# Seven-product pairs for the third block's queries, keys and values

## What is computed

```python
proj = rms_norm(x, pre_norm_w) @ w_in          # 2048 -> sb_q, sb_k, sb_v, sb_gate (1024 each),
                                               #         c_q 512, c_kv 256, k_rope 64, mla_gate 1024
o_a = stick_breaking_attention(sb_q, sb_k, sb_v)              # 8 heads of 128
o_b = chunk_causal_softmax_attention(q_mla, k_mla, v_mla)     # from c_q and c_kv, 8 heads of 192
y = concat(o_a * silu(sb_gate), o_b * silu(mla_gate)) @ w_out
return x + rms_norm(y, post_norm_w)
```

## Time and profile before

| | before |
|---|---|
| median of three runs | 1258.91 us (1258.35 to 1259.91) |
| the profiled execution, its own time | 1258.95 us |
| its span, first to last instruction | 1256.9 us |
| PE busy, matmuls | 1248.4 us (99%), 5918 |
| DVE busy | 833.9 us (66%) |
| ACT busy | 782.2 us (62%) |
| POOL busy | 205.0 us (16%) |
| mean granted clock of TensorE | 1.000 |

### The profile page before, as it was taken

One profiled execution on the slowest core, in us unless ns is written; L12 is line 12 of the kernel. 1 busy time (PEld: TensorE's weight loads), 2 busy tenths in 40 slices (PEclk: granted clock), 3 DMA queues, 4 the chain that ended last, 5 costly groups with the idle time before them and its releaser, 6 DMA issues.

```text
span 1256.9 us, 16105 instructions
## 1 busy us (share of the span) xinstructions
PE 1248.4 (99%) x5918; PEld 1040.5 (83%) x5918; DVE 833.9 (66%) x1341; ACT 782.2 (62%) x1230; POOL 205.0 (16%) x149
## 2 busy tenths in 40 slices
PE   9999999999999999999999999999999999999998
PEld 8888888888888888888888888889988888888886
DVE  5497898476657667898787765656544445576545
ACT  5798798765547556655657774456644454666543
POOL 1499999900000000000000010000000000000000
PEclk9999999999999999999999999999999999999999
DMA  9899999944566656667555545567655556655563
GB/s 348 271 256 251 271 252 247 268 159 142 184 191 184 193 184 184 201 190 213 162 157 158 155 156 199 183 181 184 178 165 164 157 161 184 195 162 161 182 194 133
DMA packets 133564, 243.85 MB, mean 194 GB/s; under 512 B 12144, under 2 KB 22512, under 8 KB 133360
## 3 DMA queue, kind: packets, MB, share of 16 engines
q1 hardware_dynamic: 129600, 229.40, 58.9%
q0 software_dynamic: 3600, 13.11, 5.3%
q10 hardware_dynamic: 288, 0.32, 0.1%
HBM read 227.60 MB, written 2.10 MB: 183 GB/s over the span
## 4 chain that ended last, share of the span: by engine, by line
PE 94%; POOL 2%; DVE 1%; ACT 1%; DMA 1%; issue 0%; DVEq 0%; ACTq 0%
PE PS L1768 28%; PE PS L1770 28%; PE PS L1769 27%; PE PS L1687 2%; PE PS L1706 2%; PE PS L1800 1%; POOL w_more L581 1%; PE PS L1802 1%; PE PS L1801 1%; PE PS L1955 1%; DMA tap_products<-tap_products 1%; POOL w_lo L581 1%; PE PS L1851 0%; PE PS L1890 0%; PE PS L1853 0%; PE PS L1852 0%
## 5 line engine op out<-in xcount | busy, mean ns | idle before, releaser
L1133 DVE TENSOR_TENSOR w_lo<-w_raw,w_hi 128x1024 fp32r<-128x1024 f32 (+2 forms) x339 | 407.9, 1205 | 300.7 <-ACT w_hi L637 299.9
L637 ACT ACTIVATE w_hi<-w_raw 128x1024 fp32r<-128x1024 f32 (+2 forms) x383 | 399.0, 1044 | 332.0 <-PE PS L1770 302.2
L1768 PE MATMUL PS<-w_hi,actB_hi 128*128 128x512 f32 (+1 forms) x736 | 292.4, 397 | 0.0
L1770 PE MATMUL PS<-w_hi,actB_lo 128*128 128x512 f32 (+1 forms) x736 | 284.8, 387 | 0.0
L1769 PE MATMUL PS<-w_lo,actB_hi 128*128 128x512 f32 (+1 forms) x736 | 284.1, 386 | 0.0
L1768 PE MATMUL PS<-w_hi,actA_hi 128*128 128x512 f32 x724 | 283.7, 392 | 0.0
L1770 PE MATMUL PS<-w_hi,actA_lo 128*128 128x512 f32 x724 | 282.1, 390 | 0.0
L1769 PE MATMUL PS<-w_lo,actA_hi 128*128 128x512 f32 x724 | 281.8, 389 | 0.0
L1770 PEld LDWEIGHTS PS<-w_hi,actB_lo 128*128 128x128 f32 x736 | 138.1, 188 | 28.8
L1770 PEld LDWEIGHTS PS<-w_hi,actA_lo 128*128 128x128 f32 x724 | 135.9, 188 | 28.8
L1769 PEld LDWEIGHTS PS<-w_lo,actB_hi 128*128 128x128 f32 x736 | 138.4, 188 | 25.6
(11 more groups left out here) (336 smaller groups left out, 1258.2 us busy)
## 6 DMA issues: line engine op xcount, KB each, us to landing
w_raw<-in_a_w_in SPq DMA_DIRECT2D x95, 512.0 KB, 5.8
w_raw<-in_w_in SPq DMA_DIRECT2D x88, 512.0 KB, 3.7
w_raw<-in_w_kv SPq DMA_DIRECT2D x64, 512.0 KB, 3.8
w_raw<-in_b_w_in SPq DMA_DIRECT2D x64, 512.0 KB, 3.8
w_raw<-in_a_w_out SPq DMA_DIRECT2D x32, 512.0 KB, 3.7
w_raw<-in_b_w_out SPq DMA_DIRECT2D x32, 512.0 KB, 3.7
w_raw<-in_w_out SPq DMA_DIRECT2D x32, 512.0 KB, 4.2
tap_products<-tap_products POOLq DMA_DIRECT2D x25, 512.0 KB, 8.3
```

Of the source, the lines that this page charges most:

```text
L637: nc.scalar.activation(split_slot(u)[0][:, f:2 * w], w_raw[:, RAW_SLOT[u], f:2 * w], ACT.Copy)\
L1133: V.tensor_tensor(wl, w_raw[:, RAW_SLOT[u], f:2 * w], wh.bitcast(F32), ALU.subtract)\
L1768: T.matmul(bank, ah, wh[:, kk, :], start=(first or opens_last and tok == 1) and kk == 0, stop=False)
L1770: ins = T.matmul(bank, al, wh[:, kk, :], start=False, stop=last and kk == 1)
```

## The change

It adds a second table, `LATE`: seven more pairs by seven products, three in sb_q (units 318, 322, 326), two in sb_k (336, 340), two in sb_v (352, 356), each with its partner unit behind it. These groups use seven PSUM banks, other ones for each group: `col1` for the first chunk, `col2` for the second, `more` for three products by themselves. The softmax heads keep to bank 6 (transposes too). For this:

- `late_acts` (DVE, steps 291 to 295, ACT in step 294): whole activations and their four sums of six K tiles, operations of 1536 or 384 elements, in parts.
- `late_differences` (DVE, steps 297 to 301, ACT in step 300, ahead of the hi parts of c_q): the difference of the two tiles of positions for the other 12 K tiles, 1536 elements each. The plain units of the second chunk of each group use it for `tok` 0 (`late_diff`), since one product of each pair is summed into the bank of `tok` 1 and is added to both.
- ACT reads one bank after a group's last pair, DVE joins (`join_late`) and scales and adds at the end (`finish_late`), in place of ACT's evacuations. For sb_v both halves are finished in step 362.
- The transposes of sb_q stand at steps 332 and 333, those of sb_k at 348 and 349, through the group's `col2`.
- The row maxima and exponentials of a softmax head stand behind the joins and the split of their step; on DVE `differences` come behind them.

The number of loads and their bytes stay. The core of the diff (the sums use `differences`, `differences_lo` and `seven_products` as they are, with other rooms; left out are the rooms, the semaphores' names and ACT's removed evacuations):

```diff
+LATE = [dict(c=C_SBQ, which="B", quads=(2, 4, 6), col1=(2, 3), col2=(0, 1), more=(4, 5, 7), turned="qu1"),
+        dict(c=C_SBK, which="B", quads=(3, 5), col1=(4, 5), col2=(2, 3), more=(7, 0, 1), turned="sq1"),
+        dict(c=C_SBV, which="B", quads=(3, 5), col1=(0, 1), col2=(4, 5), more=(7, 2, 3), turned="sk1")]
+LATE_BANKS = {}
+for g in LATE:
+    LATE_BANKS[g["c"]], LATE_BANKS[g["c"] + 1] = g["col1"], g["col2"]
+LATE_SUMS = max(len(g["quads"]) for g in LATE)
+LATE_PLAIN = 2 * min(len(g["quads"]) for g in LATE)
...
 KEEP_AT = [FIRST[C_V + 2] - 8, FIRST[C_Q] - 1]
+LATE_ACTS_AT, LATE_DIFF_AT = DONE[C_CQ - 1] + 3, DONE[C_CQ - 1] + 9
...
-BY_DVE = set(range(C_OUT, C_V)) | set(range(C_Q, C_ZB)) | set(range(C_OUTB, C_CQ)) | set(range(C_OUT2, NCH))
+BY_DVE = set(range(C_SBQ, C_MG)) | set(range(C_OUT, C_V)) | set(range(C_Q, C_ZB)) | set(range(C_OUTB, C_CQ)) | set(range(C_OUT2, NCH))
...
-            return PS[:, 2 * (c % 2) + tok, 0:(w or CHUNKS[c][2])]
+            bank = LATE_BANKS[c][tok] if c in LATE_BANKS else 2 * (c % 2) + tok
...
                         act.wait_ge(S["m_pt"], h + 1)
-                        nc.scalar.activation(probs_t[:, :], PS[:, 7, 0:384], ACT.Copy)\
+                        nc.scalar.activation(probs_t[:, :], PS[:, 6, 0:384], ACT.Copy)\
...
+                for n, g in enumerate(LATE):
+                    if u == g["units"][-1] + 2:
+                        act.wait_ge(S["units_done"], u)
+                        if n < 2:
+                            transposed(act, "sq1" if n else "ckv")
+                        for tok in range(TT):
+                            ins = nc.scalar.activation(late_join(g, 0, tok), PS[:, g["more"][0], :], ACT.Copy,
+                                                       scale=r_x2[:, tok:tok + 1])
+                        ins.then_inc(S["late_first"], 1)
...
+                h, b = divmod(u - MLA_FROM, MLA_STEP)
+                if 0 <= h < HEADS and b == 0:
+                    act.wait_ge(S["m_negmax"], h + 1)
+                    for tok, (f, e) in enumerate(((0, 128), (128, 384))):
+                        ins = nc.scalar.activation(work[:, h % 2, f:e], PS[:, 6, f:e], ACT.Exp,
+                                                   bias=neg_max[:, tok:tok + 1],
+                                                   accum_out=sums[:, tok:tok + 1])
+                    ins.then_inc(S["m_exp"], 1)
+                if u == LATE_ACTS_AT + 3:
+                    act.wait_ge(S["late_acts"], 1)
+                    chunk_done(act, C_CQ - 1)
+                    nc.scalar.activation(flat_a(hi)[:, 4 * NC:4 * NC + 512 * LATE_SUMS],
+                                         aux[:, 5 * H8:5 * H8 + 512 * LATE_SUMS], ACT.Copy)\
+                        .then_inc(S["late_acts_hi"], 1)
+                if u == LATE_DIFF_AT + 3:
+                    act.wait_ge(S["late_diff"], 1)
+                    at = 0
+                    for part in late_diffs(0):
+                        n = part.shape[-1]
+                        ins = nc.scalar.activation(part, aux[:, 4 * H8 + at:4 * H8 + at + n], ACT.Copy)
+                        at += n
+                    ins.then_inc(S["late_diff_hi"], 1)
+                for i, (m, dst, scale) in enumerate((("sq", sq_t, float(DH ** -0.5)), ("sk", sk_t, 1.0))):
+                    for j in range(2):
+                        if u == FIRST[LATE[i + 1]["c"]] + 2 + j:
+                            copy_pairs(f"{m}{j}", lambda b: dst[:, 4 * j + 2 * b:4 * j + 2 * b + 2, :], scale,
+                                       LATE[i]["col2"])
...
+            def late_acts(step):
+                n = 128 * LATE_SUMS
+                a = aux[:, 4 * H8:4 * H8 + 4 * n].rearrange("p (k t n) -> p k t n", t=TT, n=P)
+                a11, a12, a21, a22 = a[:, 0::2, 0, :], a[:, 1::2, 0, :], a[:, 0::2, 1, :], a[:, 1::2, 1, :]
+                sums_of = aux[:, 5 * H8:5 * H8 + 4 * n]
+                s1, s2, s3, s4 = (sums_of[:, i * n:(i + 1) * n].rearrange("p (q n) -> p q n", n=P) for i in range(4))
+                if step == 0:
+                    dve.wait_ge(S["lo_ready"], LO_NO["v3"] + 1)
+                    dve.wait_ge(S["on_ready"], HEADS)
+                    link(V.tensor_tensor(aux[:, 4 * H8:4 * H8 + 4 * n].rearrange("p (k s) -> p k s", s=SEQ),
+                                         hi["B"][:, 0:2 * LATE_SUMS, :].bitcast(F32),
+                                         lo["B"][:, 0:2 * LATE_SUMS, :].bitcast(F32), ALU.add))
+                if step == 1:
+                    link(V.tensor_tensor(s1, a21, a22, ALU.add))
+                    V.tensor_tensor(s3, a11, a21, ALU.subtract)
+                if step == 2:
+                    link(V.tensor_tensor(s2, s1, a11, ALU.subtract))
+                    V.tensor_tensor(s4, a12, s2, ALU.subtract).then_inc(S["late_acts"], 1)
+                if step == 4:
+                    dve.wait_ge(S["late_acts_hi"], 1)
+                    V.tensor_tensor(flat_a(lo)[:, 4 * NC:4 * NC + 4 * n], sums_of,
+                                    flat_a(hi)[:, 4 * NC:4 * NC + 4 * n].bitcast(F32), ALU.subtract)\
+                        .then_inc(S["late_acts_lo"], 1)
+            def late_differences(step):
+                n = KT - LATE_PLAIN
+                d, rest = (aux[:, at:at + P * n].rearrange("p (k n) -> p k n", n=P) for at in (4 * H8, 5 * H8))
+                if 0 <= step < 2:
+                    part = (lo if step else hi)["B"][:, LATE_PLAIN:KT, :].bitcast(F32)
+                    if step:
+                        dve.wait_ge(S["late_acts_lo"], 1)
+                    link(V.tensor_tensor(rest if step else d, part[:, :, 0:P], part[:, :, P:SEQ], ALU.subtract))
+                if step == 2:
+                    V.tensor_tensor(d, d, rest, ALU.add).then_inc(S["late_diff"], 1)
+                if step == 4:
+                    dve.wait_ge(S["late_diff_hi"], 1)
+                    at = 0
+                    for part, part_hi in zip(late_diffs(1), late_diffs(0)):
+                        w = part.shape[-1]
+                        ins = V.tensor_tensor(part, aux[:, 4 * H8 + at:4 * H8 + at + w], part_hi.bitcast(F32),
+                                              ALU.subtract)
+                        at += w
+                    ins.then_inc(S["late_diff_lo"], 1)
+            def join_late(n, g):
...
+                _, second, third = (PS[:, bank, :] for bank in g["more"])
+                dve.wait_ge(S["late_first"], n + 1)
+                note(V.scalar_tensor_tensor(j10, second, r0, j00, ALU.mult, ALU.add))
+                link(V.scalar_tensor_tensor(j01, second, r1, j01, ALU.mult, ALU.add))
+                V.scalar_tensor_tensor(j11, third, r1, j01, ALU.mult, ALU.add).then_inc(S["late_joined"], 1)
+            def finish_late(g, half):
+                r0, r1 = (r_x2[:, tok:tok + 1] for tok in range(TT))
+                j00, _, j10, j11 = (late_join(g, i, tok) for i in range(2) for tok in range(TT))
+                first, second = (PS[:, bank, :] for bank in g["col2" if half else "col1"])
+                chunk_done(dve, g["c"] + (1 if half or g["c"] == C_SBV else 0))
+                dve.wait_ge(S["dve_chain"], n_chain[0])
+                dve.wait_ge(S["late_joined"], LATE.index(g) + 1)
+                if half == 0:
+                    V.scalar_tensor_tensor(late_out(g, 0, 0), first, r0, j00, ALU.mult, ALU.add)
+                    ins = V.scalar_tensor_tensor(late_out(g, 0, 1), second, r1, j11, ALU.mult, ALU.add)
+                else:
+                    link(V.scalar_tensor_tensor(j10, second, r0, j10, ALU.mult, ALU.add))
+                    V.scalar_tensor_tensor(late_out(g, 1, 0), first, r0, j10, ALU.mult, ALU.add)
+                    ins = V.scalar_tensor_tensor(late_out(g, 1, 1), second, r1, j11, ALU.mult, ALU.add)
+                ins.then_inc(S["late_done"], 1)
...
+                for n, g in enumerate(LATE):
+                    if u == g["units"][-1] + 2:
+                        join_late(n, g)
+                    for half in range(2):
+                        if u == DONE[g["c"] + (1 if half or g["c"] == C_SBV else 0)]:
+                            finish_late(g, half)
...
+                h, b = divmod(u - MLA_FROM, MLA_STEP)
+                if 0 <= h < HEADS and b == 0:
+                    dve.wait_ge(S["m_scores"], h + 1)
+                    V.reduce_max(neg_max[:, 0:1], PS[:, 6, 0:128], AX.X, negate=True)
+                    V.reduce_max(neg_max[:, 1:2], PS[:, 6, 128:384], AX.X, negate=True)\
+                        .then_inc(S["m_negmax"], 1)
+                late_acts(u - LATE_ACTS_AT)
+                late_differences(u - LATE_DIFF_AT)
...
+                    if c - 2 in IN_LATE:
+                        n, second = divmod(c - C_SBK, 2)
+                        pe.wait_ge(S["late_done" if second else "late_joined"], 2 * n + 1 if second else n + 1)
...
+                second_late = c in IN_LATE and c != LATE[IN_LATE[c]]["c"]
+                if second_late:
```

(69 more changed lines are left out.)

74 lines of the change are left out of this document (28 added, 46 removed).

## The result

The changed kernel takes **1262.09 us** (median of 15 runs, 1260.96 to 1262.94); the kernel before took 1259.4 in the 15 runs beside them. The ratio is 1.0022, with a 95% interval of 1.0014 to 1.003: slower by 2.7 us, a little more than the 0.2% from which a difference was to be told from none. The time lies in the predicted range and 1.3 above the forecast. The profiled execution took 1261.45 us, 2.5 above the one before.

The account below looks back on a forecast made before the run. PE, busy in 99% of the span, was taken as the bound. Terms of -4.4 + 4.5 + 1.1 + 0.4 + 0.35 = +1.95 us on the profiled run of 1258.95 gave 1260.8 us, range 1256.2 to 1263.8.

Parts of the forecast that it names:

- Fewer matmuls: Seven new pairs, each 21 matmuls instead of 24, save PE time: -4.4 us.
- Part 1: Narrow stretch, steps 297 to 304: differences of activations on DVE among 1.76 us units make PE wait, +4.5 us.
- Part 2: Softmax heads whose chain meets a pair: PE waits 0.9 at step 337 and 0.2 at 344, +1.1 us.
- Part 3: Transposes of two chunks in neighbouring steps: at 332 and 333 the second eight wait for ACT's copy, +0.4 us.
- Part 4: First stick-breaking head, step 362: five DVE operations for the values stand ahead of a split, +0.35 us.
- The cover of the one-time sums: Steps 291 to 295: the lead of the splits hides the sums, cost nothing; without it 0.2 to 1.6 us, once.
- The sum: All terms together on the profiled execution: -4.4 + 4.5 + 1.1 + 0.4 + 0.35 = +1.95 us.
- The work stays hidden: Rival: added work makes PE wait nowhere, as for the six old pairs, 1254.5 us; chance 0.18.
- DVE becomes the bound: Rival: all seven pairs meeting a head's chain cost 0.9 us, plus awaited loads, 1265.5 us; chance 0.11.
- The clock falls: Rival: waits before units 303 and 304 drop PE's clock, one or two units slower, 1262.6 to 1264.3 us; chance 0.04.

Follow-up runs that it names:

- the kernel before with the differences: Kernel before plus the one-time differences of activations (steps 297 to 301) and ACT's copies, which nothing reads, no new pairs: 1264.48 us, ratio 1.004.
- the jobs exchanged: Changed kernel with differences of activations moved to steps 291 to 295 and sums of activations to 309 to 314: 1258.02 us, ratio 0.9994.
- all orders mended: Changed kernel with differences and sums exchanged, softmax heads one step earlier, DVE's second part for the values at step 363: 1255.54 us, ratio 0.997.

## Why the prediction was right

- **Fewer matmuls**, -4.4: right. 5897 matmuls, 4.76 us for a pair, 4.46 us measured when hardly an order is in the way, 4.6 by the sum of the changed kernel.
- **Part 1**, +4.5: 4.65. By its steps: 0.9 before the transposes was 1.02; +3.4 at unit 303 was 3.51; +4.5 at 304 was 4.65. A difference of 1536 elements took the 1.75 us that was interpolated. The Trainium skill (VectorE: DVE Perf Modes, "The TRN2 errata") has a formula for the duration of such an operation, from which an estimate of 1757 ns comes out; the trace agrees. The chain through ACT went as written, with the gained copies from 872.59 to 874.14 (872.6 to 874.1 was written). But the prediction did not say how much of the term hung on each queue: 1.7 us is the wait at the head of ACT's, the rest DVE's own load.
- **Part 2**, +1.1: 1.05 and 0.41, so 1.46; both were undersized, at 0.9 and 0.2.
- **Part 3**, +0.4: 0.47.
- **Part 4**, +0.35: 0.68, twice what was written. Both `keep` matmuls wait: the first for ACT's copy of the hi part, which ends at 1064.65 (PE starts at 1064.70), the second for DVE's low part, which ends at 1065.24 (PE at 1065.30). The prediction counted one chain on DVE up to its end, which is what the second of them needs, and took the start of the first, 1062.33, for it.
- **The cover of the one-time sums** held: from 280 to 300 no unit started later.
- **The sum**, +1.95: these terms give +2.66 (4.65 + 1.46 + 0.47 + 0.68 - 4.6), and 0.24 ahead of step 280 adds to it in this execution. The terms that were mis-sized are thus parts 2 and 4, by 0.7 together, part 1 by 0.15 and part 3 by 0.07, and against them the gain by 0.2: small, yet the time came out just over the bound of 0.2% that the prediction drew between "same" and "slower", to which it had given the lesser chance. On which side of that bound it fell is luck, as the interval, 0.14% to 0.3%, reaches over both. The waits of PE add up to 7.3 us, within the 4 to 8 that were named. Kernels equal up to step 290 reached step 280 between 0.57 us earlier and 1.37 later than before, so 0.24 says nothing.

The rivals. *The work stays hidden* is false for the order of the change and true for a better one: 1255.54 measured (against 1258.98 beside it), 1254.5 written. *DVE becomes the bound* is false: the same 890 us of DVE fit into a span of 1253.8. *The clock falls* is false in both profiled executions of the changed kernel. The fall was seen in both of the kernel before with the differences, and there the trace agrees with the Trainium skill's passage (TensorE: Matmul & The Clock Gate, "HAM oscillation — how this bites in real kernels"), by which idle time of the engine between groups of matmuls puts the clock back. Its price there was 0.4 to 0.7 us and not the 1.76 that I gave a unit, as a wait stood behind it. That the changed kernel was spared is not explained, so this part of the forecast was luck.

My expectations of the experiments missed three times. Making the differences later gave 1259.4 and not 1257.5, as I had not looked at what stands behind ACT's copies in the new step. I had put nothing down for the clock in the kernel before with the differences. And with the jobs exchanged I had expected no wait at steps 309 to 316, where 0.53 us was left, and 1257.4, not 1258.0.

## What to carry to other kernels

When side work is added to an engine that has room on average, go through it step by step against the shortest units of the critical engine: 7.2 us of differences on DVE (3 x 1.75, 1.22 and 0.68) cost 4.65 us among units of 1.76 us and 0.1 among units of 2.72. Where the side work of one engine is waited for by another, put that wait behind everything in the second queue whose input is already there; here this alone was worth 1.7 us. If a change that should save work comes out slower, measure the saving with the orders mended before it is thrown away.

## What was not expected of the hardware

The granted clock fell to 0.51 behind a wait of 2.2 us in one kernel, in both profiled executions, on two chips, and stayed at 1.00 behind the same wait at the same place (875.98 against 875.99) in another, also in both, although that one waited again for 1.1 us after 1.8 us of work. By the mean clocks of the other executions it is not the kernel alone that decides; what does was not found.

When the narrow waits were taken away, loads of `w_q_up` landed up to 1.7 us after ACT wanted them, and cost PE 0.5 to 0.7 at step 309 in three kernels. The one with all orders mended has two such waits of ACT, of 1.29 and 0.61 us, and no loss at that step; what spares it was not tried apart.
